# One product at a time: gate products placed singly between the recurrence's steps on TensorE

## The chip, the core and the metric

The kernel runs on 1 core of one Trainium2 chip. The metric is device time in microseconds (us) of one execution; 3 runs of the kernel before gave 1864.58, 1864.59 and 1869.19 us, a median of 1864.59 us. Less is better. TensorE (PE) multiplies, VectorE (DVE) and ScalarE (ACT) work on its results, GpSimd (POOL) and SyncE (SP) mostly issue transfers.

## What is computed

Two transformer-like blocks, one after the other, all in float32 on 512 tokens of width 1024. The part that matters here is in the second block: a recurrence over tokens in two directions (`wkv_bidir`, over 256 context and 512 latent tokens), and three gates per output column that don't depend on it.

```python
def wkv_step(S, inp):
    r, w, k, v, a, b = inp
    sa = jnp.einsum('dbhvk,dbhk->dbhv', S, a)
    S = S * w[..., None, :] + sa[..., None] * b[..., None, :] + v[..., None] * k[..., None, :]
    return S, jnp.einsum('dbhvk,dbhk->dbhv', S, r)

def merge_branches(branches, gates, w_br, w_out):
    B, L, _ = gates.shape
    g = jax.nn.sigmoid(gates.reshape(B, L, N_BRANCH, D_MODEL))
    merged = g[:, :, 0] * (branches[0] @ w_br[0])
    for n in range(1, N_BRANCH):
        merged = merged + g[:, :, n] * (branches[n] @ w_br[n])
    return merged @ w_out
```

`gates` is 512 tokens by 3072 columns of the block's input projection (depth 1024).

## The kernel before

Each engine runs one long program, written out without loops on the chip. The stages follow each other: the first block, the second block's projections and its attention, then the recurrence (`rec_tensor`, `rec_vector`, `rec_scalar`), then the merge of the three branches (`merge_tensor`), the routing and 16 passes over the experts' weights, which are read from HBM.

The recurrence is cut into 6 chunks of 128 tokens for each of the two directions. A chunk is some 25 steps on TensorE, each a short row of small products that answers to a step of VectorE or ScalarE: `p1` (decay and step size), `g1`, `g2` (products of keys with queries), `x1` `u1` ... `x5` `u5` (five levels of a triangular inverse; VectorE works on the result of each before the next can start), `kn0`, `kn1` (transposes), `gv`, `a`, `s`, `m` (the state, for each half of a chunk), `y` (output), `co`, `f`. A step is named by its direction, chunk and half: `u3.01` is level 3 of chunk 1 in direction 0. `x` and `u` steps work on 32 by 32 tiles (64 MATMUL instructions, 32 for level 5), `g`, `gv`, `a`, `s`, `m` and `y` on 64 by 64 tiles. Every float32 product is two MATMUL instructions with two weight loads (LDWEIGHTS) in the trace; a transpose is one of each.

The three gates' 24 tiles of 128 columns by 512 tokens are computed in the same stage, between the steps. A tile is 8 products of 128 by 128 weights with 128 by 512 inputs, added up in one PSUM bank (`GBANK`, bank 5, the same for all tiles). ScalarE copies a finished tile out (`gate_scalar`, with its place in the list `SCALAR_STEPS`), SP stores it to HBM; the next tile's first product waits for the copy. The weights come in half tiles of four products into three buffers (`gate_load`): a load waits until the half tile three before it is used up, which the product 3 or 7 of a tile tells (`then_inc("gw", i)`).

What TensorE does in which order is written out in `TENSOR_STEPS` (line 329 on): one word for each step, and `gate` for one turn of the generator `gate_tensor` (line 1691). In the kernel before a turn is two products (line 1701: `if k % 2`, line 1702: `yield`), and `FIRST_GATES = 3` (line 326) turns run before the recurrence's first step. `VECTOR_STEPS` and `SCALAR_STEPS` are the orders of the other two engines.

Of the kernel before, what the change touches and what calls it, by code (L numbers as in the profile page):

```python
# [322 lines left out]
MAIN_CHUNKS = [0, 1, 2, 3, 6, 7, 8, 9, 10, 11, 4, 5, *range(14, 24), 12, 13, 24, 25, *range(26, 34), *range(40, 45)]  # L323


FIRST_GATES = 3


TENSOR_STEPS = """
p1.00 p1.10 gate gate gate gate gate g1.00 gate g2.00 gate gate gate g1.10 gv.000 x1.00 a.000 kn0.00 g2.10 gate gate gv.100 u1.00 a.100 x1.10 kn0.10  # L330
kn1.00 u1.10 x2.00 gate p1.01 kn1.10 x2.10 gate p1.11 u2.00 gate x3.00 gate u3.00 gate x4.00 gate u2.10 u4.00 gate x5.00 gate x3.10 u5.00 gate gate
g1.01 s.000 u3.10 gate m.000 g2.01 gate gv.001 x4.10 a.001 x1.01 u4.10 kn0.01 s.001 u1.01 x5.10 kn1.01 gate u5.10 p1.02 g1.11 s.100 m.001 y.00 g2.11
x2.01 gate m.100 gv.010 x1.11 a.010 gv.101 kn0.11 a.101 u1.11 u2.01 kn1.11 gate x3.01 p1.12 u3.01 gate x4.01 gate x2.11 gate s.101 u4.01 u2.11 gate
m.101 x3.11 y.10 x5.01 gate gv.110 u5.01 a.110 u3.11 gate gate g1.02 s.010 x4.11 gate m.010 g2.02 gate gv.011 u4.11 a.011 x1.02 x5.11 kn0.02 s.011
gate u5.11 u1.02 kn1.02 g1.12 co.02 s.110 m.011 y.01 g2.12 m.110 x2.02 gate gv.111 gv.020 a.111 a.020 x1.12 kn0.12 s.111 p1.03 u1.12 m.111 y.11 gate
gv.120 u2.02 a.120 gate x3.02 gate u3.02 kn1.12 co.12 gate x2.12 x4.02 gate p1.13 u4.02 gate u2.12 x5.02 gate x3.12 u5.02 gate g1.03 s.020 u3.12 gate
m.020 gate g2.03 gate gate gv.021 x1.03 a.021 x4.12 kn0.03 u1.03 s.021 u4.12 kn1.03 co.03 x5.12 x2.03 gate u5.12 p1.04 g1.13 s.120 m.021 y.02 m.120
x1.13 gv.030 u2.03 a.030 u1.13 gv.121 gate a.121 x3.03 g2.13 gate s.121 gate m.121 y.12 kn0.13 gv.130 kn1.13 a.130 co.13 u3.03 x2.13 gate p1.14 x4.03
gate u2.13 u4.03 gate x3.13 x5.03 gate u3.13 u5.03 gate gate gate g1.04 s.030 x4.13 gate m.030 g2.04 gate u4.13 gv.031 x1.04 a.031 x5.13 kn0.04 gate
u5.13 s.031 u1.04 g1.14 s.130 kn1.04 co.04 gate m.130 x1.14 p1.05 gv.131 u1.14 a.131 m.031 y.03 g2.14 x2.04 gv.040 gate a.040 s.131 kn0.14 kn1.14  # L340
u2.04 gate co.14 m.131 x3.04 y.13 p1.15 u3.04 gv.140 gate a.140 x4.04 x2.14 gate u2.14 u4.04 gate x5.04 gate u5.04 gate gate x3.14 g1.05 u3.14 s.040
gate m.040 g2.05 gate x4.14 gv.041 gate u4.14 a.041 x1.05 x5.14 kn0.05 s.041 gate u5.14 u1.05 kn1.05 g1.15 s.140 co.05 x2.05 m.041 m.140 g2.15 y.04
gv.141 x1.15 a.141 kn0.15 gv.050 u1.15 s.141 a.050 kn1.15 gate co.15 x2.15 u2.05 m.141 x3.05 u2.15 y.14 x3.15 u3.05 gv.150 f.04 a.150 u3.15 x4.05 f.14
gate x4.15 gate gate gate gate gate u4.15 u4.05 f.04 x5.15 f.14 gate u5.15 x5.05 gate s.150 u5.05 gate s.050 m.150 gate gv.151 m.050 a.151 gate gv.051
s.151 a.051 gate s.051 m.151 y.15 end.1 m.051 gate y.05 end.0 gate gate gate
"""


# [30 lines left out]
def build(nc, T_):  # L379
# [17 lines left out]
    with ctx:  # L397
# [1293 lines left out]
        def gate_tensor():  # L1691
            for j, (n, m) in enumerate(GJ):
                T.wait_ge(*ps.take(GBANK, "gt", n, m))
                for k in range(8):
                    i = 2 * j + k // 4
                    if k % 4 == 0:
                        T.wait_ge(d_gw[i % 3][i])
                    T.mm(ps["gt", n, m], GP3[i % 3][:, k % 4, :], HT[:, k, :], k == 0, k == 7)
                    if k % 4 == 3:
                        T.then_inc("gw", i)  # L1700
                    if k % 2:
                        yield

        def gate_scalar(j):
            n, m = GJ[j]
# [1086 lines left out]
        def tensor_program(e):  # L2792
            T.begin(e, e is None)
            pre_tensor()
            proj1_tensor()
            att_tensor()
            out1_tensor()
            proj2_tensor()
            diff_tensor()
            proj3_tensor()  # L2800
            fin = {}
            gates = gate_tensor()
            for _ in range(FIRST_GATES):
                next(gates)
            T.wait_ge(*end4())
            for step in steps(TENSOR_STEPS):
                if step[0] == "gate":
                    next(gates)
                else:
                    rec_tensor(*step, fin)  # L2810
            merge_tensor([fin[0, 5], fin[1, 5]])
            route_tensor()
            experts_tensor(T, V, A, ps, WE, d_xg, NP, over_slots_tensor)
            T.mark("end6")
            if e is None:
                oT.begin(None, True)
                over_tensor(None)
            else:
                fork(e, over_tensor, oT)
# [298 lines left out]
```

## Time and profile before

| | |
|---|---|
| time, median of 3 runs | 1864.59 us |
| the profiled execution's own span, first to last instruction | 1876.8 us |
| recurrence in it (first `p1` to the last gate product) | 788 to 1231 us |
| TensorE busy over the span | 1717.6 us (92%) |
| VectorE, ScalarE busy | 804.7 us (43%), 518.8 us (28%) |
| HBM read | 337.47 MB |

All rows come from one profiled execution. Its span is 12 us (0.65%) longer than the median of the runs. Times in rows are us from the span's start. "PE" rows are products, "PEld" rows weight loads, which are issued by the same sequencer. A row of the timeline merges instructions of one line that follow each other; `[0.76 <-DVE arena L188]` is idle time of that engine before it, and what ended it. "issue" stands where nothing that the profile shows was waited for.

### The profile page before, as it was taken

What the parts mean: (1) busy time and instruction counts of PE and PEld (TensorE: products, weight loads), DVE (VectorE), ACT (ScalarE), POOL (GpSimd) and SP (SyncE); (2) the same over time, 40 slices, a digit from 0 to 9 for tenths busy, and PEclk for the clock granted to TensorE, in tenths of its full rate; (3) what the DMA queues carried; (4) which work ended last, traced back from release to release, by engine and by line L of the source; (5) the groups of instructions that cost most, each with busy time, mean ns of one, the idle gap of its engine ahead of it and who ended that gap; (6) DMA issues with size and microseconds to landing.
All of it is one profiled execution on the core that took longest, in us unless ns stands there. A gap on an engine that the chain in (4) does not pass through costs nothing.

```text
span 1876.8 us, 37887 instructions
## 1 busy us (share of the span) xinstructions
PE 1717.6 (92%) x16822; PEld 927.4 (49%) x16822; DVE 804.7 (43%) x1484; ACT 518.8 (28%) x983; POOL 109.4 (6%) x144
## 2 busy tenths in 40 slices
PE   5999999999999999999999999999999977778786
PEld 3444566544546555556667667544454333323332
DVE  3853144656627456355654554344462211222210
ACT  3710254311127422354453341122231110101010
POOL 0000010010000000100000000000001101010100
PEclk8999989999989999999998998899999999999998
DMA  9121376351110030042221210356569999999997
GB/s 396 76 88 47 145 287 247 145 224 69 45 45 1 23 151 0 17 170 82 77 81 50 63 56 24 114 219 221 219 239 398 416 425 415 422 413 425 417 423 279
DMA packets 48360, 359.25 MB, mean 191 GB/s; under 512 B 8325, under 2 KB 8557, under 8 KB 28736
## 3 DMA queue, kind: packets, MB, share of 16 engines
q1 hardware_dynamic: 35792, 311.51, 41.2%
q0 software_dynamic: 12400, 45.27, 7.3%
q8 instruction: 134, 2.20, 0.5%
q14 instruction: 34, 0.28, 0.0%
HBM read 337.47 MB, written 27.32 MB: 194 GB/s over the span
## 4 chain that ended last, share of the span: by engine, by line
PE 74%; DMA 16%; ACT 4%; issue 3%; DVE 2%; POOL 0%; SPq 0%; ACTq 0%; DVEq 0%; POOLq 0%
PE psum L207 71%; DMA arena<-in_w 16%; PE psum L210 3%; ACT arena L204 3%; ACT L204 1%; DVE arena L154 1%; DVE arena L180 0%; DVE arena L164 0%; DVE arena L172 0%; DVE arena L160 0%; POOL arena L141 0%; DMA arena<-in_tok 0%; DVE arena L168 0%; DVE arena L159 0%; POOL out L149 0%
## 5 line engine op out<-in xcount | busy, mean ns | idle before, releaser
L207 PE MATMUL psum<-arena 32*32 32x16 f32 (+12 forms) x16178 | 1638.1, 304 | 145.2 <-DMA arena<-in_w 73.4
L207 PEld LDWEIGHTS psum<-arena 32*32 32x32 f32 (+5 forms) x16178 | 856.0, 135 | 876.3 <-issue 764.7
L204 ACT ACTIVATE arena<-psum 128x512 f32<-128x512 f32 (+5 forms) x334 | 171.4, 513 | 871.2 <-PE psum L207 670.7
L154 DVE TENSOR_TENSOR arena<-arena,psum 128x512 f32<-128x512 f32 (+3 forms) x128 | 64.9, 507 | 402.6 <-PE psum L207 209.2
L154 DVE TENSOR_TENSOR arena<-arena 128x512 f32<-128x512 f32 (+10 forms) x315 | 191.6, 608 | 31.0 <-ACT arena L204 14.7
L204 ACT ACTIVATE arena<-arena 128x512 f32<-128x512 f32 (+10 forms) x254 | 138.8, 546 | 177.7 <-DVE arena L154 41.9
L204 ACT ACTIVATE arena<-psum,arena 128x128 f32<-128x128 f32 (+3 forms) x221 | 111.7, 505 | 275.1 <-PE psum L210 135.5
L154 DVE TENSOR_TENSOR arena<-psum,arena 128x128 f32<-128x128 f32 (+3 forms) x116 | 47.4, 409 | 154.5 <-PE psum L207 141.3
L164 DVE SCALAR_TENSOR_TENSOR arena<-arena 128x512 f32<-128x512 f32 (+7 forms) x162 | 103.5, 639 | 14.5 <-ACT arena L204 8.1
L210 PE MATMUL psum<-arena 128*128 128x128 f32 x644 | 102.6, 291 | 6.1 <-ACT arena L204 3.2
L172 DVE RECIPROCAL arena<-arena 128x1 f32<-128x1 f32 (+4 forms) x71 | 79.1, 1113 | 63.0 <-ACT arena L204 59.2
L210 PEld LDWEIGHTS psum<-arena 128*128 128x128 f32 x644 | 73.6, 146 | 64.3 <-issue 46.0
L164 DVE SCALAR_TENSOR_TENSOR arena<-psum,arena 128x512 f32<-128x512 f32 (+4 forms) x84 | 49.6, 591 | 114.8 <-PE psum L207 111.2
L204 ACT ACT_TABLE_LOAD x68 | 87.2, 1283 | 18.8 <-DMA arena<-gd 11.6
L159 DVE TENSOR_SCALAR arena<-arena 128x32 f32<-128x32 f32 (+10 forms) x126 | 39.8, 316 | 57.7 <-ACT arena L204 52.7
L184 DVE COPY_PREDICATED arena<-arena,psum 128x512 f32<-128x512 uint32 (+1 forms) x60 | 35.9, 598 | 45.4 <-PE psum L207 41.3
L168 DVE COPY arena<-psum 128x512 f32<-128x512 f32 (+4 forms) x53 | 27.8, 525 | 63.2 <-PE psum L210 35.4
L180 DVE TENSOR_REDUCE arena<-psum 128x1 f32<-128x768 f32 x32 | 30.6, 958 | 47.8 <-PE psum L207 46.0
L149 POOL DMA_INDIRECT out<-arena x16 | 25.1, 1566 | 408.6 <-DVE arena L164 139.5
L143 POOL DMA_DIRECT2D arena<-kd x28 | 21.1, 753 | 240.9 <-DVE arena L154 135.3
L143 POOL DMA_DIRECT2D mods<-arena x26 | 14.4, 557 | 312.4 <-DVE arena L154 304.2
L160 DVE TENSOR_SCALAR arena<-psum,arena 128x128 f32<-128x128 f32 x64 | 26.2, 410 | 8.5 <-PE psum L210 5.0
(49 smaller groups left out, 177.7 us busy)
## 6 DMA issues: line engine op xcount, KB each, us to landing
arena<-in_w SPq DMA_DIRECT2D x127, 2048.0 KB, 34.5
arena<-in_w SPq DMA_DIRECT2D x48, 256.0 KB, 3.1
arena<-in_w SPq DMA_DIRECT2D x12, 1024.0 KB, 36.4
arena<-kd POOLq DMA_DIRECT2D x28, 256.0 KB, 3.4
gd<-arena SPq DMA_DIRECT2D x24, 256.0 KB, 3.2
arena<-gd SPq DMA_DIRECT2D x24, 256.0 KB, 5.6
arena<-in_w POOLq DMA_DIRECT2D x2, 2048.0 KB, 9.6
kd<-arena POOLq DMA_DIRECT2D x2, 1536.0 KB, 11.0
```

Source lines behind the costliest of these rows:

```text
L143: self.e.dma_start(out, in_).then_inc(*signal)
L154: return self.ends(self.e.tensor_tensor(out, a, b, op))
L159: return self.ends(self.e.tensor_scalar(out, a, s1, None, op0))
L160: return self.ends(self.e.tensor_scalar(out, a, s1, s2, op0, op1))
L164: return self.ends(self.e.scalar_tensor_tensor(out=out, in0=a, scalar=s, in1=b, op0=op0, op1=op1))
L168: return self.ends(self.e.tensor_copy(out, a))
L172: return self.ends(self.e.reciprocal(out, a))
L180: return self.ends(self.e.tensor_reduce(out, a, AX, op, negate=negate))
L184: return self.ends(self.e.copy_predicated(out, mask, a))
L204: return self.ends(self.e.activation(out, a, func, **kw))
L207: return self.ends(self.e.matmul(out, lhs, rhs, start=start, stop=stop))
L210: return self.ends(self.e.transpose(out, a, ident))
```

## The change

A turn of `gate_tensor` is one product instead of two (the `if k % 2` goes, line 1701), `FIRST_GATES` is 6 instead of 3, so the same 6 products run ahead, and `TENSOR_STEPS` has 186 words `gate` instead of 93. The first product of each former pair stays where it was. The second stands one step of the recurrence further on, unless the next word was another pair: then the order there is unchanged. 73 second products move past one step, 20 keep their place. All other words stand in the same order, and the lists of the other engines are the same.

```diff
@@ -323,26 +323,29 @@
 MAIN_CHUNKS = [0, 1, 2, 3, 6, 7, 8, 9, 10, 11, 4, 5, *range(14, 24), 12, 13, 24, 25, *range(26, 34), *range(40, 45)]
 
 
-FIRST_GATES = 3
+FIRST_GATES = 6
 
 
 TENSOR_STEPS = """
-p1.00 p1.10 gate gate gate gate gate g1.00 gate g2.00 gate gate gate g1.10 gv.000 x1.00 a.000 kn0.00 g2.10 gate gate gv.100 u1.00 a.100 x1.10 kn0.10
-kn1.00 u1.10 x2.00 gate p1.01 kn1.10 x2.10 gate p1.11 u2.00 gate x3.00 gate u3.00 gate x4.00 gate u2.10 u4.00 gate x5.00 gate x3.10 u5.00 gate gate
-g1.01 s.000 u3.10 gate m.000 g2.01 gate gv.001 x4.10 a.001 x1.01 u4.10 kn0.01 s.001 u1.01 x5.10 kn1.01 gate u5.10 p1.02 g1.11 s.100 m.001 y.00 g2.11
-x2.01 gate m.100 gv.010 x1.11 a.010 gv.101 kn0.11 a.101 u1.11 u2.01 kn1.11 gate x3.01 p1.12 u3.01 gate x4.01 gate x2.11 gate s.101 u4.01 u2.11 gate
-m.101 x3.11 y.10 x5.01 gate gv.110 u5.01 a.110 u3.11 gate gate g1.02 s.010 x4.11 gate m.010 g2.02 gate gv.011 u4.11 a.011 x1.02 x5.11 kn0.02 s.011
-gate u5.11 u1.02 kn1.02 g1.12 co.02 s.110 m.011 y.01 g2.12 m.110 x2.02 gate gv.111 gv.020 a.111 a.020 x1.12 kn0.12 s.111 p1.03 u1.12 m.111 y.11 gate
-gv.120 u2.02 a.120 gate x3.02 gate u3.02 kn1.12 co.12 gate x2.12 x4.02 gate p1.13 u4.02 gate u2.12 x5.02 gate x3.12 u5.02 gate g1.03 s.020 u3.12 gate
-m.020 gate g2.03 gate gate gv.021 x1.03 a.021 x4.12 kn0.03 u1.03 s.021 u4.12 kn1.03 co.03 x5.12 x2.03 gate u5.12 p1.04 g1.13 s.120 m.021 y.02 m.120
-x1.13 gv.030 u2.03 a.030 u1.13 gv.121 gate a.121 x3.03 g2.13 gate s.121 gate m.121 y.12 kn0.13 gv.130 kn1.13 a.130 co.13 u3.03 x2.13 gate p1.14 x4.03
-gate u2.13 u4.03 gate x3.13 x5.03 gate u3.13 u5.03 gate gate gate g1.04 s.030 x4.13 gate m.030 g2.04 gate u4.13 gv.031 x1.04 a.031 x5.13 kn0.04 gate
-u5.13 s.031 u1.04 g1.14 s.130 kn1.04 co.04 gate m.130 x1.14 p1.05 gv.131 u1.14 a.131 m.031 y.03 g2.14 x2.04 gv.040 gate a.040 s.131 kn0.14 kn1.14
-u2.04 gate co.14 m.131 x3.04 y.13 p1.15 u3.04 gv.140 gate a.140 x4.04 x2.14 gate u2.14 u4.04 gate x5.04 gate u5.04 gate gate x3.14 g1.05 u3.14 s.040
-gate m.040 g2.05 gate x4.14 gv.041 gate u4.14 a.041 x1.05 x5.14 kn0.05 s.041 gate u5.14 u1.05 kn1.05 g1.15 s.140 co.05 x2.05 m.041 m.140 g2.15 y.04
-gv.141 x1.15 a.141 kn0.15 gv.050 u1.15 s.141 a.050 kn1.15 gate co.15 x2.15 u2.05 m.141 x3.05 u2.15 y.14 x3.15 u3.05 gv.150 f.04 a.150 u3.15 x4.05 f.14
-gate x4.15 gate gate gate gate gate u4.15 u4.05 f.04 x5.15 f.14 gate u5.15 x5.05 gate s.150 u5.05 gate s.050 m.150 gate gv.151 m.050 a.151 gate gv.051
-s.151 a.051 gate s.051 m.151 y.15 end.1 m.051 gate y.05 end.0 gate gate gate
+p1.00 p1.10 gate gate gate gate gate gate gate gate gate g1.00 gate gate g2.00 gate gate gate gate gate gate g1.10 gate gv.000 x1.00 a.000 kn0.00
+g2.10 gate gate gate gv.100 gate u1.00 a.100 x1.10 kn0.10 kn1.00 u1.10 x2.00 gate p1.01 gate kn1.10 x2.10 gate p1.11 gate u2.00 gate x3.00 gate gate
+u3.00 gate gate x4.00 gate gate u2.10 gate u4.00 gate x5.00 gate gate x3.10 gate u5.00 gate gate gate g1.01 gate s.000 u3.10 gate m.000 gate g2.01
+gate gv.001 gate x4.10 a.001 x1.01 u4.10 kn0.01 s.001 u1.01 x5.10 kn1.01 gate u5.10 gate p1.02 g1.11 s.100 m.001 y.00 g2.11 x2.01 gate m.100 gate
+gv.010 x1.11 a.010 gv.101 kn0.11 a.101 u1.11 u2.01 kn1.11 gate x3.01 gate p1.12 u3.01 gate x4.01 gate gate x2.11 gate gate s.101 gate u4.01 u2.11 gate
+m.101 gate x3.11 y.10 x5.01 gate gv.110 gate u5.01 a.110 u3.11 gate gate gate g1.02 gate s.010 x4.11 gate m.010 gate g2.02 gate gv.011 gate u4.11
+a.011 x1.02 x5.11 kn0.02 s.011 gate u5.11 gate u1.02 kn1.02 g1.12 co.02 s.110 m.011 y.01 g2.12 m.110 x2.02 gate gv.111 gate gv.020 a.111 a.020 x1.12
+kn0.12 s.111 p1.03 u1.12 m.111 y.11 gate gv.120 gate u2.02 a.120 gate x3.02 gate gate u3.02 gate kn1.12 co.12 gate x2.12 gate x4.02 gate p1.13 gate
+u4.02 gate u2.12 gate x5.02 gate x3.12 gate u5.02 gate g1.03 gate s.020 u3.12 gate m.020 gate gate g2.03 gate gate gate gate gv.021 gate x1.03 a.021
+x4.12 kn0.03 u1.03 s.021 u4.12 kn1.03 co.03 x5.12 x2.03 gate u5.12 gate p1.04 g1.13 s.120 m.021 y.02 m.120 x1.13 gv.030 u2.03 a.030 u1.13 gv.121 gate
+a.121 gate x3.03 g2.13 gate s.121 gate gate m.121 gate y.12 kn0.13 gv.130 kn1.13 a.130 co.13 u3.03 x2.13 gate p1.14 gate x4.03 gate u2.13 gate u4.03
+gate x3.13 gate x5.03 gate u3.13 gate u5.03 gate gate gate gate gate g1.04 gate s.030 x4.13 gate m.030 gate g2.04 gate u4.13 gate gv.031 x1.04 a.031
+x5.13 kn0.04 gate u5.13 gate s.031 u1.04 g1.14 s.130 kn1.04 co.04 gate m.130 gate x1.14 p1.05 gv.131 u1.14 a.131 m.031 y.03 g2.14 x2.04 gv.040 gate
+a.040 gate s.131 kn0.14 kn1.14 u2.04 gate co.14 gate m.131 x3.04 y.13 p1.15 u3.04 gv.140 gate a.140 gate x4.04 x2.14 gate u2.14 gate u4.04 gate x5.04
+gate gate u5.04 gate gate gate gate x3.14 gate g1.05 u3.14 s.040 gate m.040 gate g2.05 gate x4.14 gate gv.041 gate u4.14 gate a.041 x1.05 x5.14 kn0.05
+s.041 gate u5.14 gate u1.05 kn1.05 g1.15 s.140 co.05 x2.05 m.041 m.140 g2.15 y.04 gv.141 x1.15 a.141 kn0.15 gv.050 u1.15 s.141 a.050 kn1.15 gate co.15
+gate x2.15 u2.05 m.141 x3.05 u2.15 y.14 x3.15 u3.05 gv.150 f.04 a.150 u3.15 x4.05 f.14 gate x4.15 gate gate gate gate gate gate gate gate gate gate
+u4.15 gate u4.05 f.04 x5.15 f.14 gate u5.15 gate x5.05 gate s.150 gate u5.05 gate s.050 gate m.150 gate gv.151 gate m.050 a.151 gate gv.051 gate s.151
+a.051 gate s.051 gate m.151 y.15 end.1 m.051 gate y.05 gate end.0 gate gate gate gate gate gate
 """
 
 
@@ -1698,8 +1701,7 @@
                     T.mm(ps["gt", n, m], GP3[i % 3][:, k % 4, :], HT[:, k, :], k == 0, k == 7)
                     if k % 4 == 3:
                         T.then_inc("gw", i)
-                    if k % 2:
-                        yield
+                    yield
 
         def gate_scalar(j):
             n, m = GJ[j]
```

## Rows read from the trace of the kernel before

**Rows 1.** Busy time per stretch: us, busy and instructions of each engine, PEclk, DMA share, GB/s

```profile
788.00:1232.00 444.00, 420.43 (x11107) 282.35 (x11106) 227.45 (x446) 176.63 (x356) 34.04 (x49) 0.95 0.25 80
1232.00:1308.00 76.00, 76.00 (x184) 34.03 (x183) 31.72 (x54) 20.77 (x31) 4.64 (x7) 1.00 0.62 229
...
1400.00:1870.00 470.00, 389.52 (x1802) 154.85 (x1800) 99.57 (x246) 51.45 (x100) 39.14 (x30) 0.96 0.99 409
```

**Rows 2.** SP's timeline, 1150 to 1480: first expert weights; start, us, what

```profile
1307.83 167.52 SPq L143 DMA_DIRECT2D arena<-in_w  x30
```

**Rows 3.** TensorE's waits, 788 to 1231: total us, times, longest

```profile
PE psum L207 <- issue: 15.4, 15, 1.8
PE psum L207 <- ACT arena L204: 6.4, 5, 2.5
PE psum L210 <- issue: 1.9, 1, 1.9
```

**Rows 4.** Weight loads by time, steps with pairs between: start, us, form, count, idle before

```profile
836.21 0.95 PEld L207 LDWEIGHTS psum<-arena 32*32 32x32 f32 x66 [0.76 <-DVE arena L188]
...
838.78 0.95 PEld L207 LDWEIGHTS psum<-arena 32*32 32x32 f32 x66 [0.76 <-issue]
...
841.35 0.63 PEld L207 LDWEIGHTS psum<-arena 32*32 32x32 f32 x64 [0.76 <-issue]
```

**Rows 5.** Weight loads by time: two steps side by side, then a lone pair

```profile
843.92 1.19 PEld L207 LDWEIGHTS psum<-arena 32*32 32x32 f32 x128 [0.76 <-ACT arena L204]
846.23 0.30 PEld L207 LDWEIGHTS psum<-arena 128*128 128x128 f32 x2 [1.13 <-ACT arena L204]
...
848.15 0.92 PEld L207 LDWEIGHTS psum<-arena 32*32 32x32 f32 x34 [0.76 <-DVE arena L188]
```

**Rows 6.** Weight loads by time: two pairs in a row (852 to 856)

```profile
853.23 0.19 PEld L207 LDWEIGHTS psum<-arena 128*128 128x128 f32 x1 [0.24 <-issue]
...
854.09 0.19 PEld L207 LDWEIGHTS psum<-arena 128*128 128x128 f32 x1 [0.24 <-issue]
...
855.46 2.04 PEld L207 LDWEIGHTS psum<-arena 64*64 64x64 f32 x114 [0.76 <-DVE arena L184]
```

**Rows 7.** VectorE's last result ahead of `g1.01` (timeline)

```profile
854.77 0.44 DVE L184 COPY_PREDICATED arena<-arena,psum 128x256 f32<-128x256 uint32 x1
```

**Rows 8.** Weight loads that waited for ScalarE (timeline)

```profile
898.17 0.95 PEld L207 LDWEIGHTS psum<-arena 32*32 32x32 f32 x66 [0.88 <-ACT arena L204]
...
1112.65 0.30 PEld L207 LDWEIGHTS psum<-arena 128*128 128x128 f32 x2 [0.18 <-ACT arena L204]
```

**Rows 9.** A gate tile's copy on ScalarE (timeline)

```profile
1112.00 0.60 ACT L204 ACTIVATE arena<-psum 128x512 f32<-128x512 f32 x1 [0.85 <-PE psum L207]
```

**Rows 10.** Products by time around gaps that end in "issue"

```profile
867.34 0.33 PE L207 MATMUL psum<-arena 32*32 32x16 f32 x18 [1.75 <-issue]
867.60 0.66 PE L210 MATMUL psum<-arena 128*128 128x128 f32 x4
868.19 2.38 PE L207 MATMUL psum<-arena 64*64 64x64 f32 x106
871.07 0.37 PE L207 MATMUL psum<-arena 32*32 32x32 f32 x6 [0.50 <-issue]
...
1040.67 3.25 PE L207 MATMUL psum<-arena 32*32 32x16 f32 x128 [0.45 <-issue]
1044.25 20.30 PE L207 MATMUL psum<-arena 32*32 32x32 f32 x510 [0.33 <-issue]
1065.56 0.32 PE L207 MATMUL psum<-arena 32*32 32x32 f32 x9 [1.02 <-issue]
...
1135.18 1.01 PE L210 MATMUL psum<-arena 128*128 128x128 f32 x4 [1.94 <-issue]
```

**Rows 11.** Two stretches after such gaps (columns as in rows 1)

```profile
872.00:876.00 4.00, 4.00 (x29) 1.64 (x29) 0.00 (x0) 2.64 (x4) 0.00 (x0) 0.57 0.01 4
...
1135.00:1142.00 7.00, 6.82 (x93) 3.83 (x93) 0.08 (x1) 0.60 (x1) 0.00 (x0) 0.52 0.01 2
```

## The prediction

> **What bounds the kernel now.** I read the stretches first [rows 1]. In the recurrence, 788 to 1232 us, TensorE is busy 420.4 of 444 us, VectorE 227 and ScalarE 177: TensorE is the bound there, not the chain between the engines. In the next 76 us it is busy without a break. The experts' weights start at 1307.83 us [rows 2], behind that unbroken work, and from 1400 us on the transfers are at 0.99 of what they can do. So the end hangs on the first expert load, that load on TensorE's work, and a microsecond lost or won in the recurrence arrives at the end as one.
>
> Then the waits [rows 3]: TensorE stands still for 23.7 us in the recurrence, 17.3 of them with "issue" and 6.4 on ScalarE. Not one row names VectorE. The reader is to see two things: a better mix of steps and products can win back at most these 24 us, and the part that steps waiting for VectorE could give is zero.
>
> The profiled execution spans 1876.8 us, 12 more than the median of the runs, 1864.6. I work out differences in it and add them to the median.
>
> **Removed and moved.** No product is removed or added: 186 turns of one instead of 93 of two. What changes is how often TensorE goes over from a step to gate products and back. In the old list the word "gate" stands in 74 unbroken runs; in the new list in 131 (a run goes on over "end", which issues nothing). No old run vanishes, since first products keep their place: 57 runs are new.
>
> **The price of a run.** Inside a run a load of weights follows the last by 0.43 us, and a product has two: 0.86 us (853.23 to 854.09) [rows 6]. A lone pair that began after a wait took from 846.23 to 848.15 until the next step's first load, 1.92 us, where 2 x 0.86 = 1.72 [rows 5]. So going in and out costs 0.20 us. It shows at the way out: 0.76 us idle ahead of each such step, 0.24 within the run [rows 4, 6]. The cost doesn't hang on the run's length. The step ahead pays too if the step behind has the same tile form: an x or u step with its pair takes 2.57 us from start to start (836.21, 838.78, 841.35) [rows 4], less 1.72 that is 0.85; two such steps side by side load for 1.19 us [rows 5], one alone for 0.63 [rows 4], so the second adds 0.56. The run between them costs 0.85 - 0.56 = 0.29 us beyond its products.
>
> Of the 57 new runs, 29 stand between steps of the same family (x and u, or g, gv, a, s and m: u2.10 and u4.00, x3.10 and u5.00, g1.01 and s.000), where I take 0.29, and 28 between different ones, where I take 0.20: 8.4 + 5.6 = 14.0 us. The bounds are 57 x 0.20 = 11.4 and 57 x 0.29 = 16.5. No row shows a run of one product in this stage, so the bound from below is nothing at all (first rival). Nothing hides this cost, since it is TensorE's own.
>
> **New waits.** A step behind a run's first product now comes 0.86 us sooner relative to the work ahead of it, so it waits where its input had less than that to spare. Matching each step's start with the end of the result that it needs, I find nine such steps. g1.01: VectorE ends at 854.77 + 0.44 = 855.21 [rows 7], the step starts at 855.46 [rows 6]. It would wait 0.86 - 0.25 + 0.05 = 0.66 us. x2.11 already waits for ScalarE at 898.17 [rows 8]: 0.86 more. s.051: about 0.3. Five others (m.100, u2.13, s.101, and x3.00 and u2.10 ahead of the wait of 1.13 us at 846.23 [rows 5]) come to nothing, because they spare enough or because a wait just before or behind takes the place of theirs; so does g1.00.
>
> A tile's last product is always a second one, the next tile's first always a first one. So the step between them no longer covers ScalarE's copy. The copy takes 0.60 us [rows 9] and with its two signals about 0.70. Only one of the 23 borders loses all its cover: x5.04 leaves the place ahead of 1112.65, where the copy was only just done (1112.00 + 0.60) [rows 8, 9]; the two products now follow each other, 0.7 us. (One more, ahead of g2.00, loses it too, but ScalarE is late there with other work in any case.) The borders at 834, 959 and 1202 us lose up to 0.1 each. Sum of new waits: 0.66 + 0.86 + 0.3 + 0.7 + 0.3 = 2.8 us. Bounds: 0.7 (the border alone), and 0.7 at each of 23 borders, 16 (third rival). Behind a late copy ScalarE's a and s copies queue; the nearest, s.101's, comes 1.6 us later, and its reader m.101 had 2.1 to spare.
>
> **SP.** Loads of weights wait for products 3 and 7, both second ones, so up to a step later. Three buffers leave eight products between, at least 6.9 us, and no gate product waits for a transfer in [rows 3]. Nothing.
>
> **What the gaps give back.** The gaps with "issue" lie at whole multiples of 128 MATMULs: from 867.34 to 871.07 us are 18 + 4 + 106, from 1040.67 to 1044.25 are 128 [rows 10]. With the loads that is 256 instructions, and it took 3.73 and 3.58 us. Where 128 MATMULs hold no gate product they are done before the next 128 can be issued. The trace has 16 such gaps (15 and 1) [rows 3]. Counting words of the new list into these stretches, two bare ones get a product: those that end at 1065.56 (gap 1.02) and 1135.18 (gap 1.94) [rows 10]; about 1.0 us each is swallowed. Four more with gaps of 0.33 to 1.42 get one more run each and swallow its 0.2 to 0.3. Give back: 3.0 us. The bounds are 0 and all 17.3.
>
> The Trainium skill, "Runtime: NRT & Kernel Launch", section "Instruction fetch mechanics", says that the sequencer fetches instructions in blocks of 256 while it executes the block before, and that crossing a border is mostly hidden. The block size agrees with the 128 MATMULs and their loads; "mostly hidden" doesn't, at up to 1.94 us a gap. By it nothing would be given back, and the sum would be 16.8 us, 1881.4.
>
> **The clock.** After some gaps the granted clock is 0.57 and 0.52 in the stretches shown [rows 11], so mostly at 1.2 of 2.4 GHz. Over the recurrence it is 0.95 [rows 1], which costs at most 0.05 x 444 = 22 us. Fourteen of the 16 gaps stay, so I take next to no change, with some 4 us either way: it falls after one gap and not after another, and a slow stretch as that from 1135 to 1142 [rows 11], 7 us at half speed, is worth some 3.5.
>
> **The sum.** 14.0 + 2.8 - 3.0 = 13.8 us more. Of the 3.5 us that the slow stretch behind 1135.18 costs I take 1.4 off, since the gap ahead of it is halved: 12.4. 1864.6 + 12.4 = 1877.0 us, 0.67% slower. Own range 1869 to 1884.
>
> **The rivals.** First: the split is free. A gate product's loads run ahead under the work before, and the 0.20 belongs to something else than going over. For it: loads show as overlapped in [rows 4]. Against it: 0.76 ahead of every step behind a run. Time: 2.8 - 3.0, so 1864.4, the same. The Trainium skill would have it so: "TensorE: Matmul & The Clock Gate", section "Step-by-step: what each phase is for", lets the next weights load while the current product runs and one product's drain overlap the next one's fill. By that the term of 14.0 would be near zero.
>
> Second: the even spread keeps instructions flowing. Gaps and slow clock hold 17.3 + 22 = 39 us. If products between steps take away two thirds of it, 26 us, the kernel is 14.0 + 2.8 - 26 = 9 us faster, 1855. It decides in favour of faster from 17 us on. For it: no stretch with four products shows a gap. Against it: 14 gaps lie where no product comes.
>
> Third: ScalarE's copy opens at each border. Adjacent tiles then wait 0.7 us 23 times, with the term of 14.0: 1864.6 + 14 + 16 = 1894. Against it: 19 borders keep a step between.
>
> **Chances.** Forecast 0.76, free split 0.10, even spread 0.05, borders 0.09. A change under 0.3% (5.6 us) can't be told from none here. Of the forecast 0.03 lies under that. Slower: 0.73 + 0.09 = 0.82; same: 0.10 + 0.03 = 0.13; faster: 0.05. The range of 8 in 10 takes the forecast's own with a margin into the free split and the unsure clock: 1868 to 1885.
>
> **What would show it.** The gates' MATMULs are as many as before and 0.43 us apart; idle times of 0.76 ahead of a step number some 131 instead of 74; the last gate product ends some 13 us later, and the first expert load by as much; the gaps at the two stretches are shorter, the other 14 where they were; a wait of 0.7 on ScalarE at x5.04. Wrong, if single products cost 0.86 with their surroundings (then the step of the price fails), if the sum of "issue" falls by more than 6 us, or if waits on VectorE appear by name.

## The result, and the profile after

The changed kernel takes 1882.51 us (median of 8 runs, 1879.05 to 1887.88); the kernel before, run beside it, 1867.75 us (8 runs). The ratio is 1.0066, 95% interval 1.0042 to 1.0090: slower, by about 12.3 us (the two medians alone lie 14.8 apart). Ratios, intervals and the fits below leave out the few runs in a slower state of the chip, in which the granted clock is lower. The time lies in the predicted range, 5.5 us above the predicted 1877.0; 3.2 of the 5.5 are the kernel before, which ran at 1864.6 in the three runs that I had.

The profiled execution spans 1880.3 us (before 1876.8). Its stretches, with columns as in [rows 1]:

```profile
788.00:1232.00 444.00, 422.72 (x11065) 273.97 (x11064) 225.72 (x443) 172.00 (x345) 28.89 (x41) 0.96 0.24 78
1232.00:1308.00 76.00, 76.00 (x185) 33.99 (x184) 31.53 (x52) 21.36 (x32) 3.43 (x5) 1.00 0.64 238
1400.00:1870.00 470.00, 389.85 (x1818) 157.05 (x1820) 100.57 (x255) 52.38 (x102) 39.13 (x30) 0.96 1.00 412
```

The picture is that of [rows 1]: TensorE is the bound in the recurrence, busy without a break behind it, and the transfers are full at the end. The recurrence runs from 782.2 to 1233.7 us here, 451.5 us against 443.1 (787.8 to 1230.9). It began 5.6 us earlier because of the clock in earlier stages, which the change doesn't touch: ahead of it 37.5 us ran at the lower clock instead of 47.8. Behind it the rest takes 645.9 us before and 646.6 after, so that what the recurrence lost arrived at the end.

TensorE's waits in the recurrence after the change (line, what was waited for; total us, times, longest), to set against [rows 3]:

```profile
PE psum L207 <- issue: 14.7, 14, 3.2
PE psum L207 <- ACT arena L204: 7.0, 8, 1.9
PE psum L210 <- issue: 0.4, 1, 0.4
PE psum L207 <- DVE arena L154: 0.3, 1, 0.3
PE psum L207 <- DVE arena L184: 0.3, 1, 0.3
```

"issue" fell from 17.3 to 15.1 us, ScalarE rose from 6.4 to 7.0, and VectorE is named for the first time, with 0.6. Waits and gaps together are 1.0 us shorter than before, and still the recurrence is 8.5 us longer: the loss is in TensorE's busy time.

What a lone product costs shows in its weight loads by time (start, us, form, count, idle before). A row counts a step's 64 loads with the next product's two:

```profile
838.86 0.95 PEld L207 LDWEIGHTS psum<-arena 32*32 32x32 f32 x66 [0.87 <-ACT arena L204]
840.57 1.05 PEld L207 LDWEIGHTS psum<-arena 32*32 32x32 f32 x66 [0.76 <-DVE arena L192]
...
844.92 0.95 PEld L207 LDWEIGHTS psum<-arena 32*32 32x32 f32 x66 [0.76 <-DVE arena L168]
846.64 0.92 PEld L207 LDWEIGHTS psum<-arena 32*32 32x32 f32 x34 [0.76 <-issue]
```

u2.10 with one product takes 840.57 - 838.86 = 1.71 us, x3.10 with one 1.72. The step alone adds 0.56 beside another of its form (worked out from [rows 4, 5]), so the lone product takes 1.15 us, where one in the middle of a row takes 0.86 [rows 6]: 0.29 for going over and back, what the prediction took for steps of the same family. Over all 110 lone products of the recurrence, the time from the product's start to the next step's is 1.06 us (median), 0.20 more than inside a row; the 59 lone pairs of before take 1.91, 0.19 more than two times 0.86. So one product or two, the price is the same.

### The profile page after: what moved, and what is told of

It is laid out like the page before. It is cut to its first block, busy times and chain, and to the rows that moved or that the text cites. A ratio compares the mean times of both kernels' runs of the same rounds, so it can differ in the third digit from the quotient of the medians.

```text
span 1880.3 us, 37881 instructions
## 1 busy us (share of the span) xinstructions
PE 1720.8 (92%) x16822; PEld 919.1 (49%) x16822; DVE 804.7 (43%) x1484; ACT 518.8 (28%) x983; POOL 109.5 (6%) x144
## 4 chain that ended last, share of the span: by engine, by line
PE 75%; DMA 16%; ACT 4%; issue 3%; DVE 2%; POOL 0%; SPq 0%; DVEq 0%; ACTq 0%; POOLq 0%
PE psum L207 71%; DMA arena<-in_w 16%; PE psum L210 3%; ACT arena L204 3%; DVE arena L154 1%; ACT L204 1%; DVE arena L180 0%; DVE arena L164 0%; DVE arena L172 0%; DVE arena L160 0%; POOL arena L141 0%; DMA arena<-in_tok 0%; DVE arena L168 0%; DVE arena L159 0%; POOL out L149 0%
```

## Experiments

**How I compare them.** The times of one kernel scatter by some 10 us, and they follow the clock that TensorE was granted: a straight line through the times of all kernels against the mean granted clock of each execution, with one slope and one offset for each kernel, gives 1.26 us (plus or minus 0.16) less for each 0.001 more of the clock and leaves 3.2 us of scatter. So beside the measured ratio I give the difference at equal clock, with its 95% interval. Where an edit moves the clock itself, that part of its effect is left out there. "Runs" are unbroken runs of gate products. The diffs of the lists below show only the words around an edit.

| kernel | runs | ratio to before | at equal clock, us against before |
|---|---|---|---|
| after | 131 | 1.0066 (1.0042 to 1.0090) | +12.5 ± 2.4 |
| half | 101 | 1.0026 (0.9998 to 1.0054) | +5.9 ± 2.2 |
| shift64 | 74 | 0.9976 (0.9950 to 1.0001) | -3.8 ± 2.1 |
| after64 | 131 | 1.0121 (1.0100 to 1.0141) | +16.5 ± 3.4 |
| fill | 77 | 0.9930 (0.9902 to 0.9958), 0.9902 (0.9872 to 0.9932) | -9.7 ± 1.8 |
| fillsplit | 138 | 0.9995 (0.9964 to 1.0026) | +6.9 ± 2.6 |
| best2 | 79 | 0.9925 (0.9901 to 0.9950) | -6.7 ± 2.2 |

My theory: the loss is the number of runs times a price for going over between the steps' small tiles and the products' 128 by 128. The rivals: the split itself is free and the loss lies in where the 128-MATMUL borders fall ("borders"), or any interruption of a row of products costs, whatever its form.

### Half of the split undone: half

In 30 places, where the steps on both sides of the new run are of one family, the second product goes back to its first; runs between different families stay.

```diff
-gate gate x4.00 gate gate u2.10 gate u4.00 gate x5.00 gate gate x3.10 gate u5.00 gate gate gate g1.01 gate s.000 u3.10
+gate gate x4.00 gate gate u2.10 u4.00 gate gate x5.00 gate gate x3.10 u5.00 gate gate gate gate g1.01 s.000 u3.10
```

> The changed kernel, with 30 of the 58 moved ends undone: new runs stay only between steps of different families (x/u on one side, g, gv, a, s, m on the other, or p1, kn, co). 101 runs of gate products instead of 74 and 131. Theory (a run costs 0.20 here, with some 1.4 of the new waits and 2 given back by two gaps): 27 x 0.20 + 1.4 - 2.0 = 4.8 us over before, ratio 1.0026; the changed kernel 1.0066. Rival (going in and out is free, the loss of the change is in waits and the clock): 1.4 - 2.0, ratio 0.9997.

Measured: 1875.9 us, 1.0026; at equal clock +5.9 us for 27 more runs than before, 0.22 each, where after has +12.5 for 57, 0.22 each. So the loss fits the number of runs. By the ratio alone a free split (0.9997) lies at the very edge of the interval. The profiled execution puts the price lower: its recurrence is 442.6 us, 0.5 less than before, with 10.3 us less at the lower clock, 1.2 more of waits and 1.5 less of gaps, which leaves 3.2 to 4.9 us, 0.12 to 0.18 for each new run.

### The disputed cost by itself: dwide and dsmall

Both put one more product of 128 columns between the two products of each pair; dwide with the full 128 by 128 weights, dsmall with a 32 by 32 tile of them. The product is added to the tile's sums, so both compute other gates than the reference.

```diff
 T.mm(ps["gt", n, m], GP3[i % 3][:, k % 4, :], HT[:, k, :], k == 0, k == 7)
+if k % 2 == 0:  # dwide
+    T.mm(ps["gt", n, m][:, 0:128], GP3[i % 3][:, k % 4, :], HT[:, k, 0:128], False, False)
+if k % 2 == 0:  # dsmall
+    T.mm(ps["gt", n, m][0:32, 0:128], GP3[i % 3][0:32, k % 4, 0:32], HT[0:32, k, 0:128], False, False)
```

> The kernel before, with one more product put between the two products of each of the 93 pairs: the same 128 by 128 weights, 128 columns, added to the tile's first 128 columns (which takes them out of what the reference computes). By the gate products' 0.86 us for 512 columns its own work is a quarter, 0.21 us. My theory is that going over costs 0.20 us only where the tile size changes: from a pair's first load to its second full product 0.86 + 0.21 = 1.07 us, and the whole 20 us over before. If any product out of the row costs it, 1.27 us, and some 38 us over before.

> The same as dwide, but the product between uses a 32 by 32 tile of the weights, as an x or u step does, with the same 128 columns, added to 32 rows of the tile's first 128 columns (which takes them out of what the reference computes). My theory, a price of 0.20 us for going to another tile size and back: 0.86 + 0.21 + 0.20 = 1.27 us from a pair's first load to its second full product, some 38 us over before, 18 more than dwide. If the split is free as such and the 57 new runs cost something else (waits, the borders of 128 MATMULs), 1.07 us as in dwide and the same 20 us.

Measured, in one run each: 1891.96 and 1923.77 us, beside 1873.13 for before: 18.8 and 50.6 us more, where I expected 20 and 38. The weight loads by time from one step over its pair to the next step, in dwide:

```profile
842.27 0.95 PEld L207 LDWEIGHTS psum<-arena 32*32 32x32 f32 x66 [0.76 <-DVE arena L154]
843.47 0.19 PEld L207 LDWEIGHTS psum<-arena 128*128 128x128 f32 x1 [0.24 <-issue]
843.90 0.41 PEld L207 LDWEIGHTS psum<-arena 128*128 128x128 f32 x3 [0.24 <-issue]
845.07 1.73 PEld L207 LDWEIGHTS psum<-arena 32*32 32x32 f32 x130 [0.76 <-ACT arena L204]
```

and in dsmall:

```profile
841.33 0.95 PEld L207 LDWEIGHTS psum<-arena 32*32 32x32 f32 x66 [0.76 <-issue]
843.04 0.13 PEld L207 LDWEIGHTS psum<-arena 32*32 32x32 f32 x2 [0.76 <-issue]
843.38 0.30 PEld L207 LDWEIGHTS psum<-arena 128*128 128x128 f32 x2 [0.20 <-issue]
844.43 0.95 PEld L207 LDWEIGHTS psum<-arena 32*32 32x32 f32 x66 [0.76 <-DVE arena L154]
```

From step to step it is 2.57 us in before [rows 4], 2.80 in dwide (842.27 to 845.07) and 3.10 in dsmall (841.33 to 844.43). A full-size product of 128 columns adds 0.23, its own work of 0.21 and nothing more; the same columns on a small tile add 0.30 on top, and a second idle time of 0.76 appears ahead of the small loads. Over the 59 places of this kind it is the same: from a pair's first load to the next step's the medians are 1.91, 2.14 and 2.44 us. 93 places of 0.30 are 28 us; the two kernels differ by 31.8, of which the clock (0.965 and 0.962) accounts for 3.8. So it is the change of the tile size that costs, not the interruption. The price is above the 0.20 that I expected here and agrees with the 0.29 of the same-family runs; that this is because here too both sides are of one form is argued, not shown.

The Trainium skill has a rule that fits, which I had not weighed: "TensorEngine Tiling (Array Packing)", section "Key Properties", says that changing the tiling mode, not merely the tile, drains TensorE. It gives no duration; the traces put 0.30 us on going out to 32 by 32 and back.

### Other borders: shift64, and the split on top of it: after64

64 small MATMULs ahead of the first gate product move every 128-MATMUL border of the recurrence by half a stretch. shift64 has the order of before, after64 that of after.

```diff
+if j == k == 0:
+    for _ in range(32):
+        T.mm(ps["gt", n, m][0:32, 0:16], GP3[0][0:32, 0, 0:32], HT[0:32, 0, 0:16], True, True)
 T.mm(ps["gt", n, m], GP3[i % 3][:, k % 4, :], HT[:, k, :], k == 0, k == 7)
```

> The order of the kernel before, with 64 more small MATMULs (32 products of a 32 by 32 corner of the first gate weights, overwritten by the first gate product) ahead of the first gate product. Theory (the gaps with 'issue' are borders of instruction blocks of 128 MATMULs and 128 loads): each border comes 64 MATMULs earlier in the order of steps, so the gaps lie some half stretch from where they were: none within u4.10, s.021, u1.13, kn0.05 and u2.15, but half a block ahead or behind; within the run they are still whole multiples of 128 MATMULs apart. Time within 10 us of before, since the sizes of the gaps are dealt out anew. Rival (the gaps belong to steps, through a wait that the profile doesn't show): gaps at the same steps and of the same sizes.

> The kernel shift64 once more, timed beside after64: the order of before with the 128-MATMUL borders half a stretch elsewhere. Its one run was 11 us under the median of before, its recurrence 9 us shorter with 10 us less of the slow clock. If the place of the borders alone decides which gaps there are, it stays 4 to 8 us faster than before (0.996 to 0.998); if that one run was the clock's chance, the same as before.

> The order of after, with 64 small products' instructions ahead of the first gate product, so that the borders of 128 MATMULs fall half a stretch elsewhere, as in shift64. Counting words at these borders, one gap of shift64 (0.97 us) gets a product, one (0.69) gets a run, one (0.54) loses a product: about 0.3 us given back on balance instead of 2.3. My theory, 57 runs for 14 us and about 1 of new waits whatever the borders: 13 to 16 us more than shift64 at equal clock, some 0.5% over before. The rival, that after lost its time to where its borders fall: within 4 us of shift64.

A single run of shift64 took 1859.88 us; ten later ones have a median of 1866.47, 0.9976 of before, at equal clock (all eleven) 3.8 us faster. The order of steps and products is the same in both. Products by time in before, around u1.03 and s.021:

```profile
988.71 1.22 PE L207 MATMUL psum<-arena 32*32 32x16 f32 x76
991.74 1.46 PE L207 MATMUL psum<-arena 64*64 64x64 f32 x68 [1.81 <-issue]
```

and in shift64:

```profile
979.63 0.30 PE L207 MATMUL psum<-arena 32*32 32x16 f32 x12
982.80 2.55 PE L207 MATMUL psum<-arena 32*32 32x16 f32 x128 [2.87 <-issue]
986.56 0.29 PE L207 MATMUL psum<-arena 32*32 32x16 f32 x4 [1.20 <-issue]
```

In before the gap comes 76 MATMULs into this row, in shift64 12: it moved by the 64 that were put in, to another step, and the next one is 128 later. The gaps belong to the place in the instruction stream, not to a step. The two kernels have nearly the same sum of them (17.3 and 15.4), yet at equal clock the time moved by 3.8 ± 2.1 us. So an edit far upstream that shifts the count can by itself move the time by some microseconds; one such shift was run.

after64 is 1894.82 us; against shift64 that is 28 us more, where I expected 13 to 16 at equal clock. Its clock is lower, 0.9585 over 4 runs against 0.9650 over 11: 8 us. At equal clock 20.3 ± 3.7 us remain. In the profiled executions (of shift64 the one run beside it) the recurrence is 459.4 us against 438.1, 21.3 more, with 10.2 us more at the lower clock (3.5 to 5.1 us, as worked out in the next section); its waits:

```profile
PE psum L207 <- issue: 14.5, 13, 2.2
PE psum L207 <- ACT arena L204: 5.4, 6, 1.9
PE psum L207 <- DVE arena L154: 0.3, 1, 0.3
PE psum L207 <- DVE arena L184: 0.3, 1, 0.3
```

Against shift64's 15.4 of issue and 5.1 of ScalarE that is on balance nothing. So here 57 runs cost 16 to 18 us, 0.28 to 0.31 each. The rival "borders" (within 4 us of shift64) falls; that the medians say 4 us more than my upper bound stays open, with four runs.

### Products moved into bare stretches: fill, and the split on top of it: fillsplit

The pairs of before, but eight of them moved by some steps into stretches of 128 MATMULs that had none (ahead of x1.10, u4.10, u1.03, a.030, x5.13, x2.04, x1.05 and u2.15). ScalarE's list takes one copy later.

```diff
-gv.001 x4.10 a.001 x1.01 u4.10 kn0.01 s.001 u1.01 x5.10 kn1.01 gate gate u5.10 p1.02
+gv.001 x4.10 a.001 x1.01 gate gate u4.10 kn0.01 s.001 u1.01 x5.10 kn1.01 u5.10 p1.02
...
-gate a.021
+a.021 gate
```

> The order of the kernel before with pairs, but eight times two products stand elsewhere: in the stretches of 128 MATMULs without a product that ended in gaps of 1.44, 1.75, 1.81, 1.36, 1.02, 0.93, 1.94 and 1.74 us, taken from neighbouring stretches with four or more (one of ScalarE's copies goes one word later). Theory (a bare stretch is done before the next block of instructions is there): the eight gaps, 12.0 us, all but go; 3 more runs cost 0.7 and new waits of two steps 1.1, so 10 us less; and with the gaps up to 31 us at half clock behind five of them, at most 15 more: 1843 to 1858, ratio 0.987 to 0.995. Rival (the gaps only move to the stretches that the products left, or the issue goes on at its own rate): the same time, ratio 1.000 within 0.002.

> The kernel fill once more, as the base for fillsplit and best2 on the same chip: 0.993 of before as measured, within 0.3%.

> The change's rule applied to fill: the last product of each run of two or more stands one step further on; 138 runs of gate products instead of 77. My theory, 0.24 us for each of 61 new runs as half and after had them, and about 1 us of new waits, less up to 3 us that the gaps left in fill can give back: 12 to 16 us over fill at equal clock, 0.999 to 1.003 of before. The rival, that the split loses because of before's own gaps and borders: within 4 us of fill.

fill takes 1855.98 us in one set of ten runs and 1851.38 in another, 0.993 and 0.990 of before: it beats both kernels. Its waits in the second profiled execution:

```profile
PE psum L207 <- issue: 9.7, 11, 2.3
PE psum L207 <- ACT arena L204: 6.4, 5, 2.4
PE psum L207 <- DVE arena L154: 0.4, 1, 0.4
```

"issue" is down from 17.3 to 9.7, with three runs more than before. The eight gaps that the edit aimed at, 12.0 us, are gone but for 0.2; other gaps grew from 5.4 to some 9.5, so in part they did move on, as the rival had it. At equal clock fill is 9.7 us faster; the rest of what it wins is the clock, 0.9692 on the mean of 20 executions against 0.9639 for before (59). In the two profiled recurrences of fill 27.3 us ran at the lower clock, in that of before 47.8. That fits fewer gaps, more clock, though no run parts the two.

fillsplit applies the change's rule to fill and ends at 0.9995 of before, as expected (0.999 to 1.003). At equal clock it is 16.6 ± 2.7 us over fill for 61 more runs, 0.27 each, a little over the 12 to 16 us that I expected: the split costs the same where the gaps are smaller.

### More of the same: best2

Three more pairs moved into bare stretches of fill (ahead of a.010, u1.01 and x3.15).

```diff
-gv.010 x1.11 a.010 gv.101
+gv.010 x1.11 gate gate a.010 gv.101
...
-kn0.01 s.001 u1.01 x5.10
+kn0.01 s.001 gate gate u1.01 x5.10
...
-y.14 x3.15 u3.05
+y.14 gate gate x3.15 u3.05
```

> fill with three more pairs moved into stretches of 128 MATMULs that still have none (behind gaps of 1.16, 1.99 and 1.47 us in its trace): 4.6 us of gaps against two more runs (0.5 us) and about 0.5 of new waits on VectorE: 3 to 4 us less than fill at equal clock, 0.990 to 0.993 of before. The rival, that the gaps move on to the next bare stretch instead of closing: the same as fill.

Measured: 0.9925, inside the expected ratio, but at equal clock 3.0 ± 2.3 us slower than fill instead of 3 to 4 faster. A miss. Its waits:

```profile
PE psum L207 <- ACT arena L204: 13.9, 7, 5.1
PE psum L207 <- issue: 7.7, 8, 2.6
PE psum L207 <- DVE arena L154: 2.2, 2, 1.8
```

The gaps did fall, from 9.7 to 7.7 (the three aimed at are gone, a new one of 2.59 stands at 1181.46), but the waits on ScalarE doubled. The first product of a tile, ahead of x2.11, waited 5.1 us until 901.25 for the copy of the tile before. That tile's last product was done by 895.5, but ScalarE was at its eight activations for p1.12 (`w.12` and `p1.12` in its list) until 899.7, as its timeline shows, and the copy, the last of the three in the second row, stands behind them in its list, which I had left as it was:

```profile
896.43 3.23 ACT L204 ACTIVATE arena<-psum,arena 128x128 f32<-128x128 f32 x8
899.70 1.50 ACT L204 ACTIVATE arena<-psum 64x256 f32<-64x256 f32 x3
```

And u4.15, without the pair that had covered it, waits 1.8 us for VectorE. Both are waits that took the place of the ones removed.

## Why the prediction was right, step by step

**The end hangs on TensorE's work.** Right. The first expert load of the unbroken series started at 1307.83 us [rows 2] and starts 3.0 us later after the change, the recurrence ends 2.9 us later, and the span is 3.5 us longer. The some 13 us that the prediction named as a sign show in neither, since this recurrence began 5.6 us earlier:

```profile
1310.86 11.06 SPq L143 DMA_DIRECT2D arena<-in_w  x5
```

**The price of a run, 14.0 us.** Right, if anything a little low. In the profiled pair the recurrence is 8.5 us longer, with 1.2 us more of waits and 2.2 less of gaps. The stretches at the lower clock, added up in the clock record of the recurrence, fall from 47.8 to 34.1 us, 13.7 less. By the line fitted through the runs a microsecond at the lower level costs 0.34 us (0.001 of 1870 us are 3.74 us at half speed, for 1.26); at most it costs 0.5. So the clock gave back 4.6 to 6.9 us, and the runs cost 8.5 - 1.2 + 2.2 + 4.6 to 6.9 = 14.1 to 16.4 us, 0.25 to 0.29 each. Steps that start behind an idle time of 0.7 us or more number 136 instead of 84 (131 and 74 were said). The rival "the split is free", and with it the reading of the Trainium skill's "TensorE: Matmul & The Clock Gate", section "Step-by-step: what each phase is for", that one product's drain overlaps the next one's fill, doesn't hold where the tile size changes: 1.15 us for a lone product against 0.86. dwide shows that it does hold where the size stays.

**New waits, 2.8 us.** Too high: 1.2 on ScalarE and VectorE together. The waits that were forecast one by one came, most of them smaller. TensorE stands idle 0.69 us at x5.04 (0.7 was said), 0.24 ahead of s.051 (0.3), 0.70 ahead of x2.11 (0.86) and 0.25 ahead of g1.01 (0.66); the three borders with up to 0.1 each show next to nothing. That is 1.9 us. Three of them in the weight loads, whose idle time begins before TensorE's own (ahead of a step 0.76 of it is usual):

```profile
896.64 0.95 PEld L207 LDWEIGHTS psum<-arena 32*32 32x32 f32 x66 [1.52 <-ACT arena L204]
...
1117.47 0.30 PEld L207 LDWEIGHTS psum<-arena 128*128 128x128 f32 x2 [1.51 <-ACT arena L204]
...
1216.42 0.91 PEld L207 LDWEIGHTS psum<-arena 64*64 64x64 f32 x18 [1.07 <-ACT arena L204]
```

x3.00 and g1.00, which I let come to nothing, wait 0.56 and 0.28, but the later waits shrank by more: the one at 846.23 [rows 5] is gone, and the longest fell from 2.46 to 1.90. Those four changes take off some 0.7. The failed step is the matching by ends: at g1.01 and x2.11 it set the whole 0.86 us against the time to spare, and where an earlier wait takes the place of a later one it counted nothing. That the runs' own 0.2 to 0.3 us ahead of a step gave its input that much more time is argued, not shown. Waits on VectorE by name, which the prediction called a sign of being wrong, did appear: 0.28 ahead of g1.00 and 0.25 ahead of g1.01. But its own term for g1.01 was such a wait, so that sign contradicted the sum and tells nothing against the price.

**Give-back, 3.0 us.** 2.2 in sum, and the place of the gaps in the instruction stream is the one named. The two bare stretches that got a product gave what was said: the gap of 1.02 us at 1065.56 [rows 10] is gone (one row of products from 1059.49 to 1069.10 without a break), that of 1.94 at 1135.18 is 0.41:

```profile
865.42 0.45 PE L207 MATMUL psum<-arena 32*32 32x16 f32 x18 [3.17 <-issue]
...
1059.49 9.61 PE L207 MATMUL psum<-arena 128*128 128x512 f32 x264
...
1139.41 0.60 PE L210 MATMUL psum<-arena 128*128 128x128 f32 x4 [0.41 <-issue]
```

But the other fourteen gaps didn't stay as they were. Those of 1.42 at 963.99 and of 0.45 and 0.33 [rows 10] are gone, four of 0.17 to 0.43 are new, and the pair of gaps of 1.75 and 0.50 at 867.34 and 871.07 became one of 3.17. I can't tell the last from chance: in two executions of the one kernel fill single gaps differ by up to 0.8 us (0.34 and 1.18 at x5.03) while the sums agree (9.8 and 9.7). The size of a single gap can't be forecast to better than that. And that 128 MATMULs without a gate product are done too early is no rule: before's recurrence has 87 such stretches, 29 of them bare, and 12 of the 29 end in a gap; the other four gaps follow stretches with two products. "Mostly hidden", as the Trainium skill has it in "Runtime: NRT & Kernel Launch", section "Instruction fetch mechanics", fits the number of the borders, since 71 of the 87 show no gap; the prediction set it aside for the size of the others, and these do add up, to 7.7 to 17.9 us in one recurrence over all kernels here.

**The clock, -1.4 us.** Over all executions the mean granted clock is 0.9651 for after and 0.9639 for before, worth 1.2 x 1.26 = 1.5 us. In the size it was luck: shift64 and after64 differ by 8 us the other way.

**The sum.** 13.8 us without the clock stands against 12.5 ± 2.4, and 12.4 with it against 12.3. Waits too high by 1.6 and give-back too high by 0.8 offset each other in part. Of the rivals, the even spread would have had to take away two thirds of 39 us of gaps and slow clock; in the profiled pair it took 2.2 us of gaps and 4.6 to 6.9 of clock, and over all executions the clock gave only 1.5. fill shows that products in the bare stretches do win (7.6 us of gaps), but the change put a product into only two of them and paid for 55 other runs. ScalarE's copies opened at one border, not at 23.

## What to carry to other kernels

Keep products of one tile size together: each row of 128 by 128 products put between steps on 32 or 64 wide tiles costs its own 0.2 to 0.3 us however long it is, so splitting n rows is priced at 0.25 n before anything else is weighed. Count the instructions of the bound engine: where 128 MATMULs hold only small work, it may stand idle at the end of them (12 of 29 such stretches here), and a long product moved into such a stretch closed all eight gaps that were tried first, while others grew by about a third of that; take along the other engines' lists, or the wait comes back elsewhere. Compare kernels at equal granted clock, or two executions of one of them can differ by more than the edit.

## What the runs showed of the hardware that I had not expected

- Half a stretch of 128 MATMULs more, far upstream and with the order untouched, makes this kernel 3.8 ± 2.1 us faster at equal clock (by the ratio alone, 0.9950 to 1.0001, no change isn't quite excluded).
- The tile size, not the interruption, carries the price: 0.30 us for a 32 by 32 product between two of 128 by 128, none for one of their own size.
- The gaps and the clock go together, if not always: in ten profiled executions 41 of 54 gaps of 1 us or more had the lower clock behind them for over 1 us, and 10 of 83 shorter ones. Behind the gap of 3.17 us the granted clock was 0.52, so nearly all of the next microseconds at 1.2 of 2.4 GHz; after the gap of 1.94 had shrunk to 0.41, the stretch from 1135 to 1142, which had 0.52 in before [rows 11], shows 1.00:

```profile
866.00:872.00 6.00, 6.00 (x122) 4.35 (x121) 2.49 (x6) 1.77 (x4) 0.00 (x0) 0.52 0.02 5
1135.00:1142.00 7.00, 6.59 (x226) 4.31 (x226) 2.14 (x5) 1.35 (x3) 0.00 (x0) 1.00 0.14 42
```
